# The 64 sample columns of a two-layer recurrent trunk: full 128x128 tiles by writing them twice, and state updates as four K=32 products

## The chip, the cores and the metric

The kernel runs on one core of one Trainium2 chip. The metric is the device time of one execution in microseconds (us); the time before is 3362.74 us, the median of 3 runs (3362.27 to 3363.33). Engines: PE multiplies matrices (PEld loads its stationary operand), DVE and ACT work on vectors, POOL builds masks and issues the DMAs of the states, SP issues the DMAs of the weights.

## The reference

One inference step of a trunk of two layers, in float32. Layer 0 mixes tokens with an mLSTM, layer 1 with HGRN2; each mixer is followed by a SwiGLU of width 5632, with RMSNorm ahead of every part. The prompt has 256 tokens that start from a zero state. The sample has 8 sequences of 8 tokens, each with a state of its own. Cut to what matters here:

```
# mLSTM, 8 heads, per chunk (the sample: one chunk of 8 tokens in each of 8 sequences)
s     = (q . k) * exp(dlog - m_t)                       # causal
num   = s @ v + w_inter * (q @ C)
C_new = decay * C + einsum('bjh,bjhc,bjhv->bhcv', w, k, v)   # (128 x 256) per sequence
# HGRN2, 16 heads
oc    = s @ iv + (q * exp(A)) @ S
S_new = exp(A_last) * S + einsum('bjhc,bjhv->bhcv', k * exp(A_last - A), iv)   # (128 x 128) per sequence
```

So a state update of the sample is, for each head, eight products that each sum over only the 8 tokens of one sequence.

## The kernel before

All 320 tokens (256 of the prompt, 64 of the sample) are columns of tiles with 128 partitions. Every weight matrix is read in tiles of 128 columns, 1 MB each. ACT rounds a tile to a high part `w_hi` (line 303), DVE takes the low part `w_lo` (line 309), and PE makes three products for each of 16 row blocks (lines 319 to 321: hi.hi, hi.lo, lo.hi), 48 in all, 320 columns wide. These are called the big products here. Three tiles after one another keep ACT, DVE and PE busy at once; `w_hi` and `w_lo` have two buffers.

The mixers' own work is laid between the big products. A head of the mLSTM has six weight tiles (slots 0 to 5), a head of HGRN2 four (slots 0 to 3). Behind the big products of a slot PE runs a "tail" of small float32 products. In the loop of the mLSTM these tails are: behind slot 0 `m6` of the head before (sums for the norm, line 1427, and part of the state update, line 1390), behind slot 1 `m7` of the head before (the rest of the update) and `m1` (gate rows of this head spread over 128 partitions by a product with 8 rows of ones, lines 1364 and 1365, and k turned, line 1358), behind slot 3 `m3` (v turned), behind slot 4 `m4` (scores), behind slot 5 `m5` (numerator, denominator, prompt state, first part of the update). In HGRN2 they are: behind slot 0 `h8` and `h4`, behind slot 1 `h5`, behind slot 2 `h6`, behind slot 3 `h7`, which ends with the state update (line 1560), all for the one or two heads before.

Token blocks are 128, 128 and 64 wide. Where the sample's 64 tokens are the stationary operand, PE works with 64 of its columns (a form that the trace writes as `128*64`); where they are summed over, with 64 of its rows (`64*128`). A state update lays k into eight masked copies (`wk_seq`, `hk_seq`; DVE lines 944 and 1224, 1024 elements), multiplies each with v over 64 rows, and DVE adds the eight products to the decayed state (line 966 for C; lines 1232 and 1236 for S).

Each engine runs its instructions in the order of the code and waits on semaphores. `lo_done` releases the big products of a slot, `g_o` tells that `h7` is done, `m_C2` and `g_S` that a head's state may be stored. At the start the arena under `kT` holds `row_m`, which two small DMAs read, so DVE waits for them (`m_stored`) ahead of the first `m_evac`.

Of the kernel before, what the change touches and what calls it, by code (L numbers as in the profile page):

```python
# [19 lines left out]
P = 128  # L20
D = 2048
KT = D // P
TP = 256
NB, TB = 8, 8
TS = NB * TB
T = TP + TS
MH, MDV = 8, 256
# [66 lines left out]
def trunk(nc, x_prompt, x_sample, C_in, n_in, m_in, S_in, norm_mix_g, norm_ffn_g, norm_final_g,  # L94
# [7 lines left out]
    with ExitStack() as ctx:  # L102
# [22 lines left out]
        seq_mask = sb("seq_mask", [TS, NB])  # L125
# [32 lines left out]

        NROWS = 2 * T + NB + TS
# [19 lines left out]
        z_gate, t_gate = carve(T), carve(T)  # L179
        row_b, row_a, row_m, row_w, sum_restart, max_restart = (carve(T) for _ in range(6))  # L180
# [3 lines left out]
        kT, qT = carve(T), carve(T)  # L184
        vT, oT = carve(2, T), carve(2, T)
# [3 lines left out]
        wk_seq = carve(NB, P)  # L189
# [8 lines left out]
        row_of_head = carve(NROWS, parts=MH)  # L198
# [5 lines left out]
        hf, hg, hg_sig, hq, hk, h_logf, hA = (carve(T) for _ in range(7))  # L204
        q_exp, k0, q0, hi_T = (carve(T) for _ in range(4))
        k_exp = h_logf
        pair = carve(2, T)
# [5 lines left out]
        hk_seq = carve(NB, P)  # L213
# [19 lines left out]
        MX = bank[2:8]  # L233

# [27 lines left out]
        m_new0, m_new1, m_new2 = sem("m_new0"), sem("m_new1"), sem("m_new2")  # L262
        m_C0, m_C1, m_C2 = sem("m_C0"), sem("m_C1"), sem("m_C2")
# [9 lines left out]
        g_ikept, g_kkept, g_kseq, g_o, g_sq, g_sum, g_rstd = (sem("g_" + n) for n in ("ikept", "kkept", "kseq", "o", "sq", "sum", "rstd"))  # L273
# [149 lines left out]
        def _(pool):  # L423
# [7 lines left out]
            pool.memset(seq_mask[:, :], 1.0)  # L431
            pool.memset(penal, 0.0)
# [13 lines left out]
            tail = penal[0:TS, TP + P:].rearrange("p (b t) -> p b t", b=NB)  # L446
# [3 lines left out]
                               fill=0.0, base=0, channel_multiplier=1)  # L450
            pool.drain()
            pool.affine_select(out=seq_mask[:, :], in_=seq_mask[:, :], pattern=[[TB, NB]], compare_op=ALU.is_ge,
# [5 lines left out]
            pool.drain()  # L458
            pool.memset(restart[:, 0:TP:SEG], 0.0)
# [41 lines left out]
            def store_C(h):  # L501
                pool.wait_ge(m_C2, h + 1)
# [36 lines left out]
        def _(act):  # L539
# [39 lines left out]
            def m2(h):  # L579

                act.wait_ge(m_turned, h + 1)
                need(act, m_C2, h)
                act.activation(k_tok[:, 0:2, :], MX[2][:, 0:2 * P].rearrange("p (a b) -> p a b", a=2), ACT.Copy)
                act.activation(k_tok[0:TS, 2, :], MX[2][0:TS, 2 * P:3 * P], ACT.Copy)
# [4 lines left out]
                act.activation(att[:, 0:TP + P], att[:, 0:TP + P], ACT.Exp, scale=-1.0)  # L589
                act.activation(att[0:TS, TP + P:], att[0:TS, TP + P:], ACT.Exp, scale=-1.0).then_inc(m_weights, 1)  # L590

            def m4(h):

                act.wait_ge(m_vturned, h + 1)
                for i in range(2):
                    act.activation(v_tok[:, 0:2, i * P:(i + 1) * P],
                                   MX[2 + i][:, 0:2 * P].rearrange("p (a b) -> p a b", a=2), ACT.Copy)
                    last = act.activation(v_tok[0:TS, 2, i * P:(i + 1) * P], MX[2 + i][0:TS, 2 * P:3 * P], ACT.Copy)
                last.then_inc(m_vkept, 1)

            def m6(h):
# [6 lines left out]
                act.activation(vT, hs, ACT.Square).then_inc(m_sq, 1)  # L608
# [121 lines left out]
            def h5(h):  # L730
                act.wait_ge(g_p[0], h + 1)
                act.activation(i_tok[:, 0:2, :], MX[0][:, 0:2 * P].rearrange("p (a b) -> p a b", a=2), ACT.Copy)
                act.activation(i_tok[0:TS, 2, :], MX[0][0:TS, 2 * P:3 * P], ACT.Copy).then_inc(g_ikept, 1)
                pair_exps(h, 1)

            def h6(h):
                act.wait_ge(g_p[1], h + 1)
                act.activation(hk_tok[:, 0:2, :], MX[4][:, 0:2 * P].rearrange("p (a b) -> p a b", a=2), ACT.Copy)
                act.activation(hk_tok[0:TS, 2, :], MX[4][0:TS, 2 * P:3 * P], ACT.Copy).then_inc(g_kkept, 1)
# [74 lines left out]
        def _(dve):  # L814
# [20 lines left out]
            def gate_rows():  # L835
# [20 lines left out]
                for l in range(2):  # L856
                    last = dve.tensor_tensor(bound_cols[:, l, :], bound_cols[:, 2 + l, :], bounds[:, 0, :], ALU.subtract)
                last.then_inc(lb_diff, 1)
                dve.wait_ge(gates_capped, 1)
                dve.tensor_scalar(row_w[0:MH], t_gate[32:32 + MH], -1.0, None, ALU.mult)  # L860
                dve.tensor_scalar(row_a[0:MH], t_gate[0:MH], CAP, None, ALU.mult)
                dve.drain()
                dve.tensor_tensor_scan(row_b[0:MH], sum_restart[0:MH], row_w[0:MH], 0.0, ALU.mult, ALU.add)
                dve.drain()
                dve.tensor_tensor(row_a[0:MH], row_a[0:MH], row_b[0:MH], ALU.subtract)
                dve.drain()
                dve.tensor_copy(row_m[0:MH], row_a[0:MH])
# [12 lines left out]
                                  row_a[0:MH, TP:T].rearrange("p (b t) -> p b t", b=NB),  # L880
                                  M_end.to_broadcast((MH, NB, TB)), ALU.subtract)
# [21 lines left out]
            def keep_gate_columns():  # L903
                dve.wait_ge(rows_turned, 1)
                turned = MX[1][:, 0:2 * 3 * MH].rearrange("p (w b h) -> p w b h", w=2, b=3)
                dve.tensor_copy(gate_cols[:, :, 0:2, :], turned[:, :, 0:2, :])
                dve.tensor_copy(gate_cols[0:TS, :, 2, :], turned[0:TS, :, 2, :]).then_inc(rows_kept, 1)
                dve.drain()

            def evac_scaled(ph, n, out, scale=None, b=None):  # L910

                src = bank[(n if b is None else b)][:, 0:T]
# [751 lines left out]
```

## Time and profile before

| | |
|---|---|
| median of the runs | 3362.74 us |
| span of the profiled execution | 3362.1 us |
| PE busy | 3291.8 us, 98% of the span, 22096 matmuls |
| DVE, ACT, POOL busy | 53%, 34%, 2% |
| mLSTM: a head | 60.6 to 61.8 us, 8 heads |
| HGRN2: a head | 41.85 us, 16 heads |

The runs of the table of times lie 0.2 to 1.2 us above the span of the profiled execution, so that the two are taken as one here. A float32 product is recorded as two MATMULs, called passes here (x2 for one product); a turned block (transpose) as one. The length of one MATMUL in the trace is its latency, 270 to 590 ns, and matmuls overlap; what a group costs PE is the distance from its start to the start of the group behind it, and the text always takes that. The granted clock is given as a share of full speed: 1.00 is 2.4 GHz and 0.50 is 1.2 GHz, and nothing lies between except in a mean.

### The profile page before, as it was taken

Reading aid. Unit: us, or ns where it says so; the run is one execution under the profiler, and the core shown is the slowest. Engines: PE = TensorE matmul, PEld = TensorE weight load, DVE = VectorE, ACT = ScalarE, POOL = GpSimd, SP = SyncE. Lnnn points to the kernel's source line nnn. Section 1 sums busy time; section 2 is a strip of 40 time slices with the busy share of each in tenths; the row PEclk is TensorE's granted clock in tenths of the full one; section 3 lists DMA queues with packets and bytes.
Section 4 is the critical chain, followed back from the end, with each engine's and each line's share of the span. In section 5 each row is a group of like instructions: output and inputs, shape, how many; then the busy total and the mean of one; then the engine's idle time right before and its main releaser. Section 6 shows DMA issues by size and latency. Waiting matters only on the chain.

```text
span 3362.1 us, 54467 instructions
## 1 busy us (share of the span) xinstructions
PE 3291.8 (98%) x22096; PEld 3214.9 (96%) x22096; DVE 1797.2 (53%) x2527; ACT 1158.1 (34%) x1306; POOL 78.6 (2%) x130
## 2 busy tenths in 40 slices
PE   7999999999999999999999999998999999999998
PEld 6999998999999999999999999988999999999998
DVE  6455454555534553455666666674555445544554
ACT  4233233333223322224444444443433223222233
POOL 2000000000000000000000000000000000000000
PEclk9999999999999999999999999998999999999999
DMA  5445444555555555555544444453555555555544
GB/s 135 140 114 165 126 129 139 138 150 150 150 150 150 149 150 150 146 142 144 145 127 126 126 126 126 126 139 89 150 150 150 150 150 150 149 150 148 149 132 116
DMA packets 856557, 470.10 MB, mean 140 GB/s; under 512 B 10424, under 2 KB 846144, under 8 KB 856480
## 3 DMA queue, kind: packets, MB, share of 16 engines
q1 hardware_dynamic: 846144, 433.22, 47.2%
q0 software_dynamic: 10144, 35.74, 3.4%
q8 instruction: 55, 0.90, 0.1%
q14 instruction: 22, 0.18, 0.0%
q10 hardware_dynamic: 192, 0.06, 0.0%
HBM read 447.46 MB, written 21.53 MB: 139 GB/s over the span
## 4 chain that ended last, share of the span: by engine, by line
PE 91%; DVE 3%; ACT 2%; DVEq 1%; DMA 1%; issue 1%; SPq 0%; ACTq 0%; POOL 0%; POOLq 0%
PE bank L319 28%; PE bank L321 27%; PE bank L320 27%; PE bank L1509 2%; DVE w_lo L309 2%; ACT w_hi L303 1%; PE bank L1390 1%; PE bank L1560 1%; PE bank L1404 1%; DVEq L1234 1%; PE bank L1548 0%; PE bank L1384 0%; DMA out_dram<-arena 0%; DVE arena L1236 0%; DVE arena L1179 0%
## 5 line engine op out<-in xcount | busy, mean ns | idle before, releaser
L319 PE MATMUL bank<-h_hi,w_hi 128*128 128x320 f32 x4608 | 1455.5, 316 | 13.5 <-DVE w_lo L309 12.3
L321 PE MATMUL bank<-h_hi,w_lo 128*128 128x320 f32 x4608 | 1428.5, 310 | 0.0
L320 PE MATMUL bank<-h_lo,w_hi 128*128 128x320 f32 x4608 | 1428.5, 310 | 0.0
L309 DVE TENSOR_TENSOR w_lo<-raw,w_hi 128x2048 fp32r<-128x2048 f32 (+1 forms) x416 | 935.6, 2249 | 494.8 <-ACT w_hi L303 494.8
L303 ACT ACTIVATE w_hi<-raw 128x2048 fp32r<-128x2048 f32 (+1 forms) x416 | 780.0, 1875 | 760.4 <-PE bank L321 756.7
L319 PEld LDWEIGHTS bank<-h_hi,w_hi 128*128 128x128 f32 x4608 | 870.1, 189 | 27.1 <-DVE w_lo L309 16.9
L320 PEld LDWEIGHTS bank<-h_lo,w_hi 128*128 128x128 f32 x4608 | 870.3, 189 | 0.2
L321 PEld LDWEIGHTS bank<-h_hi,w_lo 128*128 128x128 f32 x4608 | 869.4, 189 | 0.0
L319 PE MATMUL bank<-g_hi,w_hi 128*128 128x320 f32 x1920 | 599.8, 312 | 13.0 <-DVE w_lo L309 6.6
L320 PE MATMUL bank<-g_lo,w_hi 128*128 128x320 f32 x1920 | 596.0, 310 | 0.0
L321 PE MATMUL bank<-g_hi,w_lo 128*128 128x320 f32 x1920 | 596.0, 310 | 0.0
L914 DVE TENSOR_TENSOR arena<-bank,rstd 128x320 f32<-128x320 f32 x264 | 129.5, 490 | 479.4 <-PE bank L321 467.9
L319 PEld LDWEIGHTS bank<-g_hi,w_hi 128*128 128x128 f32 x1920 | 363.2, 189 | 17.0 <-DVE w_lo L309 7.6
L320 PEld LDWEIGHTS bank<-g_lo,w_hi 128*128 128x128 f32 x1920 | 363.1, 189 | 0.0
L321 PEld LDWEIGHTS bank<-g_hi,w_lo 128*128 128x128 f32 x1920 | 362.9, 189 | 0.0
L682 ACT ACTIVATE arena<-arena 128x320 f32<-128x320 f32 x88 | 41.6, 472 | 490.8 <-DVEq L1086 490.8
L1050 DVE TENSOR_TENSOR x<-x,bank 128x320 f32 (+1 forms) x128 | 62.4, 488 | 242.2 <-PE bank L321 242.2
L339 ACT ACTIVATE h_hi<-x,gains (+1 forms) x64 | 36.0, 563 | 205.5 <-DVEq L1055 195.2
L1509 PE MATMUL bank<-arena 128*128 128x128 f32 (+1 forms) x576 | 84.0, 281 | 0.1
L1509 PEld LDWEIGHTS bank<-arena 128*128 128x128 f32 (+1 forms) x576 | 69.7, 180 | 11.2 <-DVE arena L1156 0.3
L1164 DVE COPY_PREDICATED arena<-level_mask,bank 128x256 f32<-128x256 int8 x112 | 50.6, 452 | 34.9 <-PE bank L1509 27.9
L349 DVE SCALAR_TENSOR_TENSOR h_lo<-x,gains,h_hi (+1 forms) x64 | 35.3, 551 | 50.1 <-ACT h_hi L339 50.0
(280 smaller groups left out, 1780.5 us busy)
## 6 DMA issues: line engine op xcount, KB each, us to landing
raw<-in_ffn_w_up_dram SPq DMA_DIRECT2D x176, 1024.0 KB, 5.7
raw<-in_ffn_w_down_dram SPq DMA_DIRECT2D x64, 1024.0 KB, 6.0
raw<-in_hgrn_w_in_dram SPq DMA_DIRECT2D x64, 1024.0 KB, 6.5
raw<-in_mlstm_w_in_dram SPq DMA_DIRECT2D x48, 1024.0 KB, 5.9
raw<-in_ffn_w_down_dram SPq DMA_DIRECT2D x32, 768.0 KB, 5.1
raw<-in_mlstm_w_out_dram SPq DMA_DIRECT2D x16, 1024.0 KB, 6.1
raw<-in_hgrn_w_out_dram SPq DMA_DIRECT2D x16, 1024.0 KB, 6.1
raw<-in_state_mlstm_C_dram POOLq DMA_DIRECT2D x8, 1024.0 KB, 8.8
```

The source lines that it names most:

```text
L303: act.activation(w_hi[:, s % 2, 0:ph.k * P], raw[:, s % ph.ring, 0:ph.k * P], ACT.Copy).then_inc(hi_done, 1)
L309: dve.tensor_tensor(w_lo[:, s % 2, 0:ph.k * P], raw[:, s % ph.ring, 0:ph.k * P], w_hi[:, s % 2, 0:ph.k * P].bitcast(F32), ALU.subtract).th ...
L319: pe.matmul(out, tile_hi, hi[:, k, :], start=(k == 0), stop=False)
L320: pe.matmul(out, tile_hi, lo[:, k, :], start=False, stop=False)
L321: last = pe.matmul(out, tile_lo, hi[:, k, :], start=False, stop=(k == ph.k - 1))
L339: act.activation(h_hi[:, bass.ds(j, 1), :], x[:, bass.ds(j, 1), :], ACT.Copy, scale=gains[:, bass.ds(NORM_GAIN[r] + j, 1)]).then_inc(x_hi_ ...
L349: dve.scalar_tensor_tensor(h_lo[:, bass.ds(j, 1), :], x[:, bass.ds(j, 1), :], gains[:, bass.ds(NORM_GAIN[r] + j, 1)], h_hi[:, bass.ds(j, 1 ...
L682: act.activation(f_sig[:, (s - 1) // 2, :], fa[:, (s - 1) // 2, :], ACT.Sigmoid).then_inc(f_sig_done, 1)
L914: return dve.tensor_tensor(out, src, rstd[:, :], ALU.mult)
L1050: add = dve.tensor_tensor(x[:, bass.ds(j, 1), :], x[:, bass.ds(j, 1), :], bank[s % ph.banks][:, 0:T].rearrange("p (a t) -> p a t", a=1), A ...
L1164: dve.copy_predicated(scores[:, 0:TP], level_mask[:, li, 0:TP], MX[mx][:, 0:TP])
L1509: last = pe.matmul(MX[mx][0:c1 - c0, c0:c1], left[:, c0:c1], right[:, c0:c1], start=True, stop=True)
```

## The change

The sample's columns are written twice into the tiles of k, v, `hk`, `k0`, `pair` and i, so that the third token block is 128 wide (64 tokens and the same 64 again, or zeros). Every small product then uses all 128 rows and columns. Where the second copy would be summed as well, the masked weights or scores are zero there. The gate rows are spread from a tile with 128 partitions of which 120 are zero.

The state update no longer masks k eight times. The 128 rows of the third block are taken as four quarters of 32 rows, that is of four sequences; a quarter holds two sequences that it serves. v (or i) is laid out twice side by side, each copy masked by `half_mask` to one of the two, and one product over 32 rows gives the updates of both sequences, 512 (or 256) columns wide. The four products read different quarters of the rows and write different PSUM banks. `m7` on PE is gone, the whole update of C stands in `m6`. DVE adds decay and product in one instruction for each sequence in HGRN2 too. `row_m` lies elsewhere, and DVE waits for `m_stored` only after the loop.

```diff
-        wk_seq = carve(NB, P)
+        v_half = carve(2 * MDV)
-        row_of_head = carve(NROWS, parts=MH)
+        row_of_head = carve(NROWS)
+        row_m = carve(T)
+        NEW_C, NEW_S = (0, 2, 3, 5), (0, 1, 2, 3)
+        def group(g):
+            return slice(32 * g, 32 * g + 32)
+        def sequence(g, u):
+            return 4 * (g % 2) + 2 * (g // 2) + u
...
+            def evac_twice(out, b, scale=None):
+                evac_scaled(out[:, 0:T], b, scale)
+                return evac_scaled(out[:, T:TW], b, scale, slice(TP, T))
...
             def m5(h):      # DVE
+                for u in range(2):
+                    last = dve.tensor_scalar(v_half[:, u * MDV:(u + 1) * MDV], v_tok[:, 2, :], half_mask[:, u:u + 1], None, ALU.mult)
...
-                    if s == 1 and isinstance(it, int):
-                        dve.wait_ge(m_stored, 32)
...
             def m1(h):      # PE
-                pe.matmul(MX[0][:, 0:R_EM], ones[0:MH, :], row_of_head[:, 0:R_EM], start=True, stop=True)
+                pe.matmul(MX[0][:, 0:R_EM], ones[:, :], row_of_head[:, 0:R_EM], start=True, stop=True)
...
-            def new_C(mx, b0):
-                for i in range(2):
-                    last = pe.matmul(MX[mx][:, i * MDV:(i + 1) * MDV], wk_seq[0:TS, b0 + i, :], v_tok[0:TS, 2, :],
-                                     start=True, stop=True)
+            def new_C():
+                for g in range(ROW_GROUPS):
+                    last = pe.matmul(MX[NEW_C[g]][:, 0:2 * MDV], wk[group(g), 2, :], v_half[group(g), :], start=True, stop=True)
...
             def m6(h):      # PE
-                pe.wait_ge(m_C0, h + 1)
-                new_C(4, 2)
-                new_C(5, 4).then_inc(m_new1, 1)
-            def m7(h):
-                pe.wait_ge(m_C1, h + 1)
-                new_C(4, 6).then_inc(m_new2, 1)
+                pe.wait_ge(m_vhalf, h + 1)
+                need(pe, m_C1, h)
+                new_C().then_inc(m_new1, 1)
...
             def h7(h):      # PE
-                for b in range(NB):
-                    last = pe.matmul(MX[(0, 2)[b // 4]][:, b % 4 * P:(b % 4 + 1) * P], hk_seq[0:TS, b, :], i_tok[0:TS, 2, :],
-                                     start=True, stop=True)
+                for g in range(ROW_GROUPS):
+                    last = pe.matmul(MX[NEW_S[g]][:, 0:2 * P], hk_tok[group(g), 2, :], i_half[group(g), :], start=True, stop=True)
...
             def h8(h):      # DVE
-                dve.tensor_tensor(S, S, q_exp[:, TP + TB - 1:T:TB].rearrange("p (b a) -> p b a", a=1).to_broadcast((P, NB, P)),
-                                  ALU.mult)
-                dve.drain()
-                for i, mx in enumerate((0, 2)):
-                    last = dve.tensor_tensor(S[:, 4 * i:4 * i + 4, :], S[:, 4 * i:4 * i + 4, :],
-                                             MX[mx][:, :].rearrange("p (b v) -> p b v", b=4), ALU.add)
+                for g in range(ROW_GROUPS):
+                    for u in range(2):
+                        b = sequence(g, u)
+                        end = TP + b * TB + TB - 1
+                        last = dve.scalar_tensor_tensor(S[:, b, :], S[:, b, :], q_exp[:, end:end + 1],
+                                                        MX[NEW_S[g]][:, u * P:(u + 1) * P], ALU.mult, ALU.add)
```

Where instructions move, on PE in the loop of the mLSTM: the tails behind slot 0 and slot 1. A row is a line of the code with its operands and the output's partitions x columns. First before, line 1390 being the state update:

```order
L1427 MATMUL bank<-arena,ones 128x320 x2
L1390 MATMUL bank<-arena 128x256 x4
...
L1390 MATMUL bank<-arena 128x256 x2
L1362 REGISTER_ALU
L1364 MATMUL bank<-arena,ones 128x392
L1365 MATMUL bank<-arena,ones 128x320
L1358 MATMUL bank<-ident,arena 128x128 x2
L1358 MATMUL bank<-ident,arena 64x128
```

and the same place in the changed program, where line 1428 is the state update:

```order
L1463 MATMUL bank<-arena,ones 128x320 x2
L93 REGISTER_ALU
L1428 MATMUL bank<-arena 128x512 x4
...
L1397 REGISTER_ALU
L1400 MATMUL bank<-arena,ones 128x392
L1401 MATMUL bank<-arena,ones 128x320
L1393 MATMUL bank<-ident,arena 128x128 x3
```

The update of the tail behind slot 1 is gone, the one behind slot 0 has four products of 512 columns where four of 256 stood (two more stood in `m5`), and the turned block of 64 partitions is one of 128.

On DVE, the place in the loop of HGRN2 that runs when `h7` is done, before (`h8` and the start of `h4`):

```order
L914 TENSOR_TENSOR arena<-bank,rstd 128x320
L309 TENSOR_TENSOR w_lo<-raw,w_hi 128x2048
L1231 COPY arena<-bank 128x128
L1232 TENSOR_TENSOR arena<-arena 128x1024
L1236 TENSOR_TENSOR arena<-arena,bank 128x512 x2
L1179 SCALAR_TENSOR_TENSOR arena<-restart,arena 128x320
```

and after:

```order
L938 TENSOR_TENSOR arena<-bank,rstd 128x320
L938 TENSOR_TENSOR arena<-bank,rstd 128x64
L325 TENSOR_TENSOR w_lo<-raw,w_hi 128x2048
L1262 COPY arena<-bank 128x128
L1267 SCALAR_TENSOR_TENSOR arena<-arena,bank 128x128 x8
L1209 SCALAR_TENSOR_TENSOR arena<-restart,arena 128x320
```

Eight instructions of 128 elements stand where three of 1024, 512 and 512 stood.

## Rows read from the trace of the kernel before

**Rows 1.** The page: span, and busy time of the engines.
```profile
span 3362.1 us, 54467 instructions
PE 3291.8 (98%) x22096; PEld 3214.9 (96%) x22096; DVE 1797.2 (53%) x2527; ACT 1158.1 (34%) x1306; POOL 78.6 (2%) x130
```
**Rows 2.** Waits of PE (who waited for whom: total us, times, longest).
```profile
PE bank L1364 <- DVE arena L930: 7.4, 1, 7.4
```
**Rows 3.** Timeline of DVE at the start (start us, us, operation, [idle before]).
```profile
65.67 0.49 DVE L915 SCALAR_TENSOR_TENSOR arena<-bank,rstd 128x320 f32<-128x320 f32 x1 [4.16 <-DMA out_dram<-arena]
```
**Rows 4.** Timeline of PE, HGRN2, tail behind slot 3.
```profile
1754.13 0.39 PE L1554 MATMUL bank<-arena 128*128 128x128 f32 x2
1754.36 0.39 PE L1555 MATMUL bank<-arena 128*128 128x128 f32 x2
1754.67 0.43 PE L1556 MATMUL bank<-arena 64*128 64x64 f32 x2
1755.03 0.71 PE L1558 MATMUL bank<-arena 128*128 128x128 f32 x4
1755.68 2.05 PE L1560 MATMUL bank<-arena 64*128 64x128 f32 x16
1757.65 0.42 PE L319 MATMUL bank<-h_hi,w_hi 128*128 128x320 f32 x1
```
**Rows 5.** Timeline of PE, HGRN2, tail behind slot 2.
```profile
1742.39 2.67 PE L1509 MATMUL bank<-arena 128*128 128x128 f32 x18
1744.98 0.42 PE L319 MATMUL bank<-h_hi,w_hi 128*128 128x320 f32 x1
```
**Rows 6.** Timeline of PE, mLSTM, tail behind slot 5.
```profile
229.09 0.59 PE L1384 MATMUL bank<-arena,ones 128*128 128x256 f32 x2
235.52 0.41 PE L319 MATMUL bank<-h_hi,w_hi 128*128 128x320 f32 x1
```
**Rows 7.** Timeline of PE, mLSTM, state update behind slot 0.
```profile
243.83 1.99 PE L1390 MATMUL bank<-arena 64*128 64x256 f32 x8
245.75 0.41 PE L319 MATMUL bank<-h_hi,w_hi 128*128 128x320 f32 x1
```
**Rows 8.** Timeline of PE, mLSTM, tail behind slot 1.
```profile
252.99 1.13 PE L1390 MATMUL bank<-arena 64*128 64x256 f32 x4
254.04 0.92 PE L1364 MATMUL bank<-arena,ones 8*128 8x392 f32 x2
254.81 0.70 PE L1365 MATMUL bank<-arena,ones 8*128 8x320 f32 x2
255.74 0.39 PE L319 MATMUL bank<-h_hi,w_hi 128*128 128x320 f32 x1
```
**Rows 9.** Timelines of DVE, ACT and PE in slot 2 of the same head.
```profile
254.15 0.87 DVE L966 SCALAR_TENSOR_TENSOR raw<-raw,spread,bank 128x256 f32<-128x256 f32 x2 [0.41 <-PE bank L1390]
256.02 0.39 ACT L583 ACTIVATE arena<-bank 128x256 f32<-128x256 f32 x1 [9.21 <-PE bank L1358]
263.15 0.41 PE L319 MATMUL bank<-h_hi,w_hi 128*128 128x320 f32 x1
```
**Rows 10.** Windows (A:B, length, PE busy, granted clock, DMA share, GB/s).
```profile
193.70:197.10 3.40, 3.40 (x14) 0.50 1.04 293
242.66:263.15 20.49, 20.36 (x122) 1.00 0.52 160
180.85:202.61 21.76, 21.76 (x122) 0.92 0.49 151
```
**Rows 11.** Timelines of DVE and PE, HGRN2, slot 0.
```profile
1758.07 1.22 DVE L1232 TENSOR_TENSOR arena<-arena 128x1024 f32<-128x1024 f32 x1
1760.57 0.82 DVE L1179 TENSOR_TENSOR_SCAN arena<-restart,arena 128x320 f32<-128x320 f32 x1
1765.58 2.29 DVE L309 TENSOR_TENSOR w_lo<-raw,w_hi 128x2048 fp32r<-128x2048 f32 x1 [0.90 <-ACT w_hi L303]
1767.93 0.41 PE L319 MATMUL bank<-h_hi,w_hi 128*128 128x320 f32 x1 [0.64 <-DVE w_lo L309]
```

More of the change, by code:

```diff
@@ L26 @@
 T = TP + TS
+ROW_GROUPS = 4
+TW = T + TS
 MH, MDV = 8, 256
@@ L431, in _ @@
             pool.memset(seq_mask[:, :], 1.0)
+            pool.memset(quarters, 1.0)
             pool.memset(penal, 0.0)
@@ L450, in _ @@
                                fill=0.0, base=0, channel_multiplier=1)
+            starts = [[-80, 2], [-32, 2], [-TB, 2]]
+            pool.affine_select(out=quarters, in_=quarters, pattern=starts, compare_op=ALU.is_ge,
+                               fill=0.0, base=0, channel_multiplier=1)
             pool.drain()
+            pool.affine_select(out=quarters, in_=quarters, pattern=[[-step, n] for step, n in starts], compare_op=ALU.is_ge,
+                               fill=0.0, base=TB - 1, channel_multiplier=-1)
             pool.affine_select(out=seq_mask[:, :], in_=seq_mask[:, :], pattern=[[TB, NB]], compare_op=ALU.is_ge,
@@ L1348, in rows_to_columns @@
                 for which, row in ((0, row_a), (1, row_w)):
-                    for b, n in enumerate((P, P, TS)):
-                        last = pe.transpose(MX[1][0:n, which * 3 * MH + b * MH:which * 3 * MH + (b + 1) * MH],
-                                            row[0:MH, b * P:b * P + n], ident[0:MH, 0:MH])
+                    for b in range(3):
+                        src = row[0:MH, b * P:(b + 1) * P]
+                        last = pe.transpose(MX[1][:, which * 3 * MH + b * MH:which * 3 * MH + (b + 1) * MH],
+                                            src, ident[0:MH, 0:MH])
                 last.then_inc(rows_turned, 1)
             def turn(mx, src, inc=None):
-                for b, n in enumerate((P, P, TS)):
-                    last = pe.transpose(MX[mx][0:n, b * P:(b + 1) * P], src[:, b * P:b * P + n], ident[:, :])
+                for b in range(3):
+                    part = src[:, b * P:(b + 1) * P]
+                    last = pe.transpose(MX[mx][:, b * P:(b + 1) * P], part, ident[:, :])
                 return last
@@ L1445, in m_body @@
                         m6(before)
-                    if s == 1 and before is not None:
-                        m7(before)
                     if s in (1, 3, 4, 5):
@@ L1508, in level_products @@
                     if c0 < w:
-                        last = pe.matmul(MX[mx][0:c1 - c0, c0:c1], left[:, c0:c1], right[:, c0:c1], start=True, stop=True)
+                        keys = left[:, c0:c0 + P]
+                        last = pe.matmul(MX[mx][:, c0:c1], keys, right[:, c0:c1], start=True, stop=True)
                 return last
```

199 lines of the change are left out of this document (104 added, 95 removed).

## The prediction

> **What bounds the kernel now.** I read the page first: PE is busy for 98% of the span [rows 1]. So this change pays where it shortens what PE does, or ends one of the few waits of PE. The page's busy time can't say what a small product costs, since matmuls overlap. For that I read PE's timeline and take distances from start to start. Then I asked at each slot whether the big products behind a tail start because PE is free or because `w_lo` has come.
>
> The reader is to see three things. First, a full 128x128 pass costs 0.11 us (L1554 to L1555, two passes in 0.23), and so do the 64-row passes of L1560 (16 in 1.97, less what follows); a change of shape costs extra. L1555's two passes take 0.31 to the 64-row L1556, 0.09 over 0.22; L1556's take 0.36, 0.14 over; L1558's four full ones 0.65 for 0.45; L1560's sixteen 1.97 for 1.79 [rows 4]. Each change of form costs some 0.19 us, half ahead of the first pass and half ahead of the second. Second, the mLSTM is bound by PE, but slot 3 at 263.15 starts just as a chain ends that runs from the turned k over ACT's copies and table load, `w_hi` and `w_lo`; ACT starts it at 256.02 [rows 9]. Third, HGRN2's slot 1 starts 0.64 us after PE was free, and the chain is DVE's and ACT's from `h7`'s end at 1757.65 to 1767.93 [rows 4, 11]. At the start PE waits 7.4 us for the gate rows, and inside it DVE waits 4.16 us for a DMA [rows 2, 3].
>
> **The change part by part.** A pass of up to 128 columns is 0.112 us. A 256-column one is 0.216, (1.92 - 0.19)/8 from L1390 x8 [rows 7]; one of 392 is 0.33, (0.77 - 0.10)/2 [rows 8]. From these two a 512-column pass is 0.43, an estimate.
>
> *HGRN2, slot 2.* 18 passes in 2.59 us [rows 5] hold three blocks with 64 columns. All full: 18 x 0.112 = 2.02. Gain 0.57 a head. Slot 1 has one such block of three: a third of that, less 0.07 for passes that the wider stationary operand brings from 0.09 to 0.11: 0.12.
>
> *HGRN2, slot 3.* From L1554 to the end 3.52 us. Ahead of the update stand then ten full passes (L1554, 1555, 1556, 1558): 1.12. The update has 4 products of 2 passes, 256 columns, over 32 rows; the trace shows no 32-row product in another quarter than the one before it. Upper bound: they run one behind the other like L1390's eight passes, 1.92 + 0.09 for the change of form. That gives 3.13, a gain of 0.39. Lower bound: products on different quarters of the rows run side by side. The two passes of one product use the same quarter and stay in order, passes start in order, so pass 2 of one runs beside pass 1 of the next: five steps for eight, 5 x 0.216 + 3 x 0.03 + 0.28 = 1.45. Total 2.57, gain 0.95. I take the lower: the four banks and the four quarters are separate, and nothing else orders them. 15 heads run so.
>
> *HGRN2, slot 0.* From `h7`'s end to slot 1 are 10.28 us, of which PE waits 0.64 [rows 4, 11]; its own side is at most 9.64. As long as the chain stays above that, only the chain counts. It holds L1232 and two L1236, 2.50 us from 1758.07 to 1760.57; after it eight instructions of 128 elements. A 256-element one of that kind steps 0.39 (two in 0.87, the last 0.48 long) [rows 9]; DVE takes 1.04 ns an element (2048 in 2.29, 1024 in 1.22 [rows 11]), so 0.26 for 128; 8 x 0.26 = 2.06. Gain 0.44, 14 times. Were there no overlap between them, 0.34 each, it would be a loss of 0.24. The second copy of `k0`, 0.13 to 0.22 us, lies beside ACT: DVE waits 0.90 us for `w_hi` behind it [rows 11]. The second copy of i comes ahead of `g_o`, where DVE idles. After that the chain is 9.84. HGRN2: 15 x (0.57 + 0.12 + 0.95) + 14 x 0.44 = 30.8.
>
> *mLSTM, slots 3 to 5.* `m5` takes 6.43 us [rows 6]. After: three times 2 x 0.216 + 4 x 0.112 = 0.88 for the causal products, 0.22 for `qn`, 0.86 and 0.40 and 0.22 for the prompt's state, n and the sample's n, 4.34. Gain 2.09, part of it the piece of the update that moves to `m6`. `m4` has one 64-column block, gain 0.13; the two turned blocks of `m3` cost 0.08 more, an estimate. 2.14 x 8 = 17.1.
>
> *mLSTM, tails behind slots 0 and 1.* Behind slot 0: 1.92 [rows 7] becomes 0.19 + X. One behind the other X is 8 x 0.43 = 3.44, a loss of 1.71; side by side 5 x 0.43 + 0.08 = 2.23, a loss of 0.50. Behind slot 1: 2.75 + 0.09 [rows 8] becomes 2 x 0.33 + 2 x 0.27 + 3 x 0.11 = 1.53, gain 1.31. PE would gain 0.81. But then the wait for slot 3 grows. Now ACT's chain is released by `m_C1`: DVE is free at 253.74 [rows 9], 0.13 later with the second copy of k, and makes four instructions of 0.39 instead of two: 255.5. From there 7.13 us as before, less 0.15 for two merged ACT copies: 262.5 for 263.15. I take 0.7, and 7 heads make 4.9. In the other case PE is the later one (263.25): a loss of 0.1 each.
>
> *The clock.* In 4 of the 6 heads between 119.05 and 487.51 a stretch of 3.4 us runs at 0.50, right behind the tail of slot 1 with its 64-row and 8-row products: the same part of a head takes 21.76 us with it and 20.49 without [rows 10]. Half of that tail goes and the rest uses all rows, so I expect these stretches gone: 4 x 1.27 and 0.3 for a later, partly hidden one, 5.4.
>
> *The start and the ends.* DVE's 4.16 us wait goes off the path; against it stand 0.25 for second copies in the gate rows and 0.2 for that of k: 3.7 gained. The memset of `row_of_head` hides under ACT's gate functions. Head 0's `m1`: 0.3. In the last mLSTM head DVE no longer waits for a second set of products before the state may be stored and the tile under C loaded: 1.3. The last heads of HGRN2 wait on the same chains as slot 0, twice: 1.5, an estimate.
>
> Sum: 30.8 + 17.1 + 4.9 + 5.4 + 3.7 + 0.3 + 1.3 + 1.5 = 65.0. The profiled execution's 3362.1 us less this are 3297.1; the median of the runs stands 0.6 above that execution: **3298 us**.
>
> **The rivals.**
>
> *One behind the other.* The 32-row products don't overlap. For it: every pass in the trace waits its turn, even when the form is the same. Against it: those all use the same rows. HGRN2 gains 15 x (0.57 + 0.12 + 0.39) + 6.2 = 22.4, the mLSTM 17.1 - 0.7, the rest 12.2: 51, or **3312 us**; if 3.7 us of 32-row passes behind slot 0 also keep a half-rate stretch of 1.27 in each of seven heads, 3320.
>
> *Closer packing.* The first passes of all four products run together and then the second ones, two steps for five: 3 x 0.216 = 0.65 less in each HGRN2 head, 15 x 0.65 = 9.7. The mLSTM gains nothing further, its slot 3 waits for `m_C1`'s chain. **3288 us**. For it: nothing but the code's order ties pass 2 of one product ahead of pass 1 of the next. Against it: in every group of the trace passes start in the order in which they are issued. The Trainium skill, page "TensorE: Matmul & The Clock Gate", section "Measured speedup vs the span model", gives 3.07x for four K=32 products of 512 columns, where my five steps for eight are 1.6x; no row before the change shows it, and by it the time would be near this rival's.
>
> *Slower.* The clock. A 32-row block of 3.7 us in each mLSTM head and one of 2.0 in each HGRN2 head bring PE's clock to 0.50 for stretches like the one of [rows 10], where each costs up to 1.7. With nothing overlapping and the old stretches gone the gain is 51; 30 stretches more eat it. Two in each of 22 heads are 75: **3386 us**. For it: the stretch behind slot 1 follows narrow products. Against it: the 64-row block of 1.92 behind slot 0 [rows 7] is followed by full clock in the same head [rows 10], and HGRN2's update never lowers it.
>
> *DVE's eight instructions don't overlap*, 0.34 each: slot 0 loses 0.24 instead of gaining 0.44, 14 x 0.68 = 9.5 us: **3307 us**.
>
> **How the numbers follow.** Forecast 0.55; one behind the other 0.2; closer packing 0.1; DVE's eight 0.1; slower 0.03; the rest, no change, 0.02. The forecast's own range is 3291 to 3305, from the clock (5), the start (2 either way, as PE's idle time there is also followed by half rate) and the ends. For 8 in 10 the range goes from 3286, past closer packing, to 3318, over the serial case. A measurement tells 0.2%, 6.7 us, from no change. Faster takes all cases but two: 0.96; same 0.01; slower 0.03.
>
> **What the profile would show.** The update in HGRN2: four products from first start to big product, 1.45 us if side by side, 2.0 if not; start distances within a product of 0.216, between products of 0.03 or 0.216. In slot 2, 18 passes in 2.02. A head of HGRN2 in 39.8 us. The chain of slot 0 at 9.84 us with a wait of some 0.2 left over. In the mLSTM the update in 2.4 us, a wait of DVE's `w_lo` ahead of slot 3 in every head, heads of 57.8 us, clock 1.00 throughout. At the start a wait of PE of 3.7 us instead of 7.4. I am wrong if the passes step by 0.216 throughout, if a full third block costs more than 0.112 a pass, or if DVE or ACT come late in slots 1 to 3 of HGRN2, where PE doesn't wait for them now.

## The result, and the profile after

The changed kernel takes 3282.86 us, the median of 4 runs (3280.78 to 3284.13), beside 3363.0 for the kernel before (4 runs, 3362.27 to 3363.33): a ratio of 0.9761, with a 95% interval of 0.9748 to 0.9774. The forecast was 3298 with a range of 3286 to 3318: the direction was right and the gain, 80 us, larger than the range allowed. The profiled execution went from 3362.1 to 3279.3 us, by 82.8 where the sum said 65.0.

The page of the changed kernel, span and busy time, which answers to [rows 1]:

```profile
span 3279.3 us, 54117 instructions
PE 3201.8 (98%) x21904; PEld 3152.9 (96%) x21904; DVE 1778.3 (54%) x2619; ACT 1155.3 (35%) x1242; POOL 79.2 (2%) x135
```

PE is still the bound at 98%, with 192 fewer matmuls of 22096. Most of the gain is thus in the distances between matmuls, not in their number. Timeline of PE, HGRN2, the tail behind slot 3 (start us, length us, then the instruction), which answers to [rows 4]:

```profile
1633.53 0.38 PE L1583 MATMUL bank<-arena 128*128 128x128 f32 x2
1633.75 0.39 PE L1584 MATMUL bank<-arena 128*128 128x128 f32 x2
1633.97 0.39 PE L1585 MATMUL bank<-arena 128*128 128x128 f32 x2
1634.20 0.33 PE L1586 MATMUL bank<-arena 128*128 128x64 f32 x2
1634.37 0.66 PE L1588 MATMUL bank<-arena 128*128 128x128 f32 x4
1634.96 0.71 PE L1590 MATMUL bank<-arena 32*128 32x256 f32 x8
1635.61 0.41 PE L335 MATMUL bank<-h_hi,w_hi 128*128 128x320 f32 x1
```

L1590 is the state update: eight passes of 256 columns fit between 1634.96 and 1635.61, 0.65 us. Passes that queue behind one another start 0.216 us apart at this width; such a distance is called a step here, and eight steps would be 1.73. Two more terms: a quarter is 32 of the 128 rows, and a change of form is the place where PE goes from products over 128 rows to products over 32 or back. Two narrower cuts of the same timeline show how they lie:

```profile
1634.96 0.50 PE L1590 MATMUL bank<-arena 32*128 32x256 f32 x4
...
1635.28 0.39 PE L1590 MATMUL bank<-arena 32*128 32x256 f32 x4
```

The four first passes all start at 1634.96 (within 0.02 us), the four second ones at 1635.28. From L1584 to the big product are 1.86 us, where before L1554 to L319 took 3.52 [rows 4]: a gain of 1.66, and the prediction had 0.95. The tail behind slot 2, which answers to [rows 5], is a timeline of PE as well:

```profile
1661.55 2.12 PE L1538 MATMUL bank<-arena 128*128 128x128 f32 x18
1663.48 0.39 PE L335 MATMUL bank<-h_hi,w_hi 128*128 128x320 f32 x1
```

It is 1.93 us long, where it was 2.59 and 2.02 was forecast. Slot 0 of HGRN2, timelines of DVE and, in the last line, of PE, which answer to [rows 11]:

```profile
1636.06 2.15 DVE L1267 SCALAR_TENSOR_TENSOR arena<-arena,bank 128x128 f32<-128x128 f32 x8
1638.12 0.82 DVE L1209 TENSOR_TENSOR_SCAN arena<-restart,arena 128x320 f32<-128x320 f32 x1
...
1643.13 2.29 DVE L325 TENSOR_TENSOR w_lo<-raw,w_hi 128x2048 fp32r<-128x2048 f32 x1 [0.77 <-ACT w_hi L319]
...
1645.48 0.42 PE L335 MATMUL bank<-h_hi,w_hi 128*128 128x320 f32 x1 [0.36 <-DVE w_lo L325]
```

DVE's eight instructions step by 0.26 us (2.06 for all), as forecast, and from the end of `h7` (1635.61) to slot 1 (1645.48) are 9.87 us against 10.28 before; 9.84 was forecast. The timeline writes a wait of 0.36 for PE.

The mLSTM: the update behind slot 0, and the tail behind slot 5, timeline of PE, which answer to [rows 7] and [rows 6]:

```profile
215.56 0.59 PE L1421 MATMUL bank<-arena,ones 128*128 128x256 f32 x2
...
219.86 0.39 PE L335 MATMUL bank<-h_hi,w_hi 128*128 128x320 f32 x1
...
228.15 0.71 PE L1428 MATMUL bank<-arena 32*128 32x512 f32 x4
...
228.68 0.61 PE L1428 MATMUL bank<-arena 32*128 32x512 f32 x4
229.22 0.42 PE L335 MATMUL bank<-h_hi,w_hi 128*128 128x320 f32 x1
```

`m5` takes 4.30 us (4.34 forecast, 6.43 before). The whole update of C takes 1.07 us, again two steps. Slots 2 and 3 of the same head, timelines of ACT, DVE and PE, which answer to [rows 9]:

```profile
239.98 0.49 ACT L608 ACTIVATE arena<-bank 128x384 f32<-128x384 f32 x1 [8.84 <-DVE raw L997]
...
240.80 1.28 ACT L610 ACT_TABLE_LOAD   x1
...
242.69 1.90 ACT L319 ACTIVATE w_hi<-raw 128x2048 fp32r<-128x2048 f32 x1
...
244.63 2.29 DVE L325 TENSOR_TENSOR w_lo<-raw,w_hi 128x2048 fp32r<-128x2048 f32 x1 [1.47 <-ACT w_hi L319]
...
238.37 0.41 PE L335 MATMUL bank<-h_hi,w_hi 128*128 128x320 f32 x1 [0.32 <-DVE w_lo L325]
...
246.97 0.42 PE L335 MATMUL bank<-h_hi,w_hi 128*128 128x320 f32 x1 [1.30 <-DVE w_lo L325]
```

DVE's update of C (L997) releases ACT at 239.98; three copies, a table load and an exponential stand ahead of ACT's `w_hi` for slot 3, and DVE's `w_lo` follows it. By the timeline PE has been free for 1.30 us when slot 3 starts. The waits of PE for the whole program (who waited for whom: total us, times, longest) say the same: before, `w_lo` cost PE 18.9 us in 18 waits, now more.

```profile
PE bank L335 <- DVE w_lo L325: 28.6, 32, 4.2
...
PE bank L1400 <- DVE arena L962: 3.5, 1, 3.5
```

The second row answers to [rows 2]: 7.4 us became 3.5. Last the windows of PE (A:B, length, PE busy, granted clock, DMA share, GB/s), a whole mLSTM head, the six behind it and the start:

```profile
111.28:169.30 58.02, 56.30 (x384) 1.00 0.52 148
169.30:514.65 345.35, 335.63 (x2283) 1.00 0.51 145
63.10:66.50 3.40, 3.40 (x8) 0.50 0.49 61
```

The half-rate stretches of [rows 10] are gone from the seven mLSTM heads between the first and the last mark of the table below. Behind the gate rows at the start 3.4 us still run at 0.50; before it was 10.2 us:

```profile
64.00:74.20 10.20, 7.50 (x23) 0.50 0.31 68
```

Read by the marks of the timeline (first product of the norm's sums in each head) the 82.8 us lie as follows. The forecast column is the prediction's terms, sorted by the same marks; eight heads have seven stretches between their marks, sixteen have fifteen.

| stretch | before | after | gained | forecast |
|---|---|---|---|---|
| to the first mLSTM mark | 119.05 | 111.28 | 7.8 | 6.1 |
| 7 mLSTM heads | 429.36 | 403.37 | 26.0 | 25.3 |
| to the first HGRN2 mark | 1132.69 | 1128.10 | 4.6 | 2.9 |
| 15 HGRN2 heads | 615.98 | 572.25 | 43.7 | 30.6 |
| rest | 1065.02 | 1064.3 | 0.7 | 0 |

Most of the miss, 13.1 of 17.8 us, is in HGRN2, whose head went from 41.85 to 38.85 us. The first and the third row are known less well than the others. Six traces of kernels whose instructions up to the first mLSTM mark are the same (this one, q0000, q0011, q0101, k128 and narrow below) reach it between 108.26 and 111.28 us. The third row's stretch takes 1127.72 to 1130.03 us in three traces with the same instructions in it (this one, stored and rows8). One trace tells these two rows to 2 or 3 us only.

### The profile page after: what moved, and what is told of

Read it like the earlier page. It is cut to its first block, busy times and chain, and to the rows that moved or that the text cites. A ratio compares the mean times of both kernels' runs of the same rounds, so it can differ in the third digit from the quotient of the medians.

```text
span 3279.3 us, 54117 instructions
## 1 busy us (share of the span) xinstructions
PE 3201.8 (98%) x21904; PEld 3152.9 (96%) x21904; DVE 1778.3 (54%) x2619; ACT 1155.3 (35%) x1242; POOL 79.2 (2%) x135
## 4 chain that ended last, share of the span: by engine, by line
PE 90%; DVE 5%; ACT 3%; issue 1%; DMA 1%; DVEq 0%; SPq 0%; ACTq 0%; POOL 0%; POOLq 0%
PE bank L335 28%; PE bank L337 27%; PE bank L336 27%; DVE w_lo L325 2%; PE bank L1538 2%; ACT w_hi L319 1%; DVE arena L1267 1%; PE bank L1441 1%; PE bank L1577 0%; DVE raw L997 0%; PE bank L1421 0%; DVE arena L1209 0%; PE bank L1590 0%; DMA arena<-in_mlstm_w_in_dram 0%; PE bank L1357 0%
## 5 line engine op out<-in xcount | busy, mean ns | idle before, releaser
L319 ACT ACTIVATE w_hi<-raw 128x2048 fp32r<-128x2048 f32 (+1 forms) x416 | 780.3, 1876 | 746.3 <-PE bank L337 741.0
L938 DVE TENSOR_TENSOR arena<-bank,rstd 128x320 f32<-128x320 f32 (+1 forms) x296 | 133.5, 460 | 486.0 <-PE bank L337 476.0
L1538 PE MATMUL bank<-arena 128*128 128x128 f32 (+1 forms) x576 | 73.0, 277 | 0.0
L1538 PEld LDWEIGHTS bank<-arena 128*128 128x128 f32 x576 | 69.5, 194 | 0.0
L1196 DVE COPY_PREDICATED arena<-level_mask,bank 128x320 f32<-128x320 int8 (+1 forms) x112 | 55.0, 491 | 24.1 <-PE bank L1538 16.7
```

Of the source, the lines that this page charges most:

```text
L319: act.activation(w_hi[:, s % 2, 0:ph.k * P], raw[:, s % ph.ring, 0:ph.k * P], ACT.Copy).then_inc(hi_done, 1)
L938: return dve.tensor_tensor(out, src, rstd[:, cols], ALU.mult)
L1196: dve.copy_predicated(scores[:, 0:w], level_mask[:, li, 0:w], MX[mx][:, 0:w])
L1538: last = pe.matmul(MX[mx][:, c0:c1], keys, right[:, c0:c1], start=True, stop=True)
```

## Experiments

**Which products overlap.** If quarters of the rows are what lets the four products run at once, putting two or all four on the same quarter must bring steps back, and full rows must bring all eight. In all four kernels of this group only the operands' rows change, in both updates (L1428 and L1590), so the instructions and the work around them stay. The new states of the sample then lack some of their sums or have sums of other sequences in them. The diff shows the two operands of the product alone.

```diff
-    wk[group(g), 2, :], v_half[group(g), :]             # and the same for hk_tok, i_half
+    wk[group(0), 2, :], v_half[group(0), :]             # q0000
+    wk[group(g // 2), 2, :], v_half[group(g // 2), :]   # q0011
+    wk[group(g % 2), 2, :], v_half[group(g % 2), :]     # q0101
+    wk[:, 2, :], v_half[:, :]                           # k128
```

> The changed kernel, but all four 32-row products of both state updates read rows 0 to 31 (so the new states are wrong sums; everything else is computed). Theory A, packing: products on different quarters of the rows run at the same time, products on the same quarter one behind the other. Then HGRN2's update takes 0.19 + 8 x 0.216 = 1.92 us instead of 0.64, 15 x 1.28 = 19 us more; the mLSTM's 0.19 + 8 x 0.43 = 3.6 instead of 1.07, of which 1.9 us a head are hidden by the waits ahead of slots 2 and 3, so 7 x 0.6 = 4 us more; in all 3283 + 23 = 3306. Rival B: a 32-row pass is short wherever it reads, the quarters don't matter: 3283, HGRN2's update stays at 0.64. Rival C: in addition the clock drops to 0.50 behind the 3.6 us block in the mLSTM: some 7 us on top, 3313.

> The changed kernel, but products 0 and 1 read rows 0 to 31 and products 2 and 3 rows 32 to 63 (wrong sums in the new states). Theory A with free order: what counts is how many passes share a quarter, four here: 4 steps of 0.216, HGRN2's update 1.05 to 1.15 us, 15 x 0.43 = 6.5 us more, 3289. Rival D, the order of issue counts: pass starts stay in order, products 2 and 3 can't begin until product 1's last pass has: 7 steps, 1.8 us, 15 x 1.1 = 17 more, 3300.

> As the run before, with quarters 0, 1, 0, 1. Theory A with free order: four passes on each of two quarters, 4 steps, the same 3289. Rival D, order of issue: the pairs stand well here; if the passes of a product are issued one behind the other, 0a 0b 1a 1b, product 1 begins beside 0b: 7 steps for the eight passes, if all first passes of a pair go out before the second ones, 4 steps. A difference between this run and the one before shows that order counts, none that it doesn't.

> The changed kernel, but the four products of both updates read all 128 rows (wrong sums in the new states): full tiles without quarters, no change of form anywhere in the loops. Theory A: HGRN2's update 8 x 0.216 = 1.73 us ahead of the big products, against 0.64 and 0.12 for changes of form: 15 x 1.0 = 15 us more. mLSTM: 3.44 against 1.16, less 1.9 that the waits hide: 7 x 0.4 = 3 us more. 3301; and 5 us less than the run with all products on quarter 0, by the changes of form. Rival B: as fast as the changed kernel.

Measured: q0000 3306.67 us (ratio 0.9834, 0.9818 to 0.9851), q0011 3289.93 (0.9782, 0.9765 to 0.9798), q0101 3288.11 (0.9778, 0.9761 to 0.9794), k128 3301.39 (0.9819, 0.9802 to 0.9835), the kernel before 3361.77 on the same chip. In q0000 the second pass starts 0.32 us behind the first, the six others 0.216 apart, and the big product 0.31 behind the last. Timelines of PE around the update, q0000:

```profile
1719.88 1.99 PE L1590 MATMUL bank<-arena 32*128 32x256 f32 x8
1721.80 0.41 PE L335 MATMUL bank<-h_hi,w_hi 128*128 128x320 f32 x1
```

q0011, whole and in a narrow cut that holds only the first starts:

```profile
1717.26 1.14 PE L1590 MATMUL bank<-arena 32*128 32x256 f32 x8
1718.33 0.42 PE L335 MATMUL bank<-h_hi,w_hi 128*128 128x320 f32 x1
...
1717.26 0.49 PE L1590 MATMUL bank<-arena 32*128 32x256 f32 x2
```

and k128:

```profile
1719.33 1.89 PE L1590 MATMUL bank<-arena 128*128 128x256 f32 x8
1720.87 0.49 PE L335 MATMUL bank<-h_hi,w_hi 128*128 128x320 f32 x1
```

The block is 0.65 us on four quarters, 1.07 on two and 1.92 on one. With 0.216 for a step these are 2, 4 and 8 steps and each time some 0.2 for the change of form inside the block (0.43 + 0.2, 0.86 + 0.2, 1.73 + 0.2). So the products of one quarter queue among themselves, and products of different quarters start within 0.02 us of each other. Two quarters take the same time in the order 0,0,1,1 and in the order 0,1,0,1. In q0011 two passes start together at 1717.26; passes of one quarter can't (q0000), so the second is of the third product or the fourth, and it starts ahead of the second product. The order in the code isn't what decides.

k128 has eight steps without a change of form, but its 1.54 us read too short. The big product starts 0.03 behind the last pass there, and the second big product 0.33 behind the first, where 0.25 lie between them in q0000. From the start of L1588, the group ahead of the update, to the second big product are 2.38 us in k128 and 2.76 in q0000: the change of form to 32 rows and the one back cost 0.39 together. The block's own distance holds 0.2 of that, the groups on either side the rest. k128 also shows what packing as such is worth over a kernel with full rows: 18.5 us by the medians of the two kernels, beside which the kernel before took 3361.77 and 3363.0. HGRN2's heads take 38.85, 39.27, 40.1 us (4, 2, 1 quarters) and 39.9 (k128).

**What the mLSTM's update is worth.** In q0000 the update of C takes 2.56 us longer as well (3.63 for 1.07), yet a head of the mLSTM is only 0.7 us longer (58.43 for 57.7): the waits ahead of slots 2 and 3 take it up. Two kernels try that. order_mh takes the waits away by order alone; all work is kept. ACT makes the `w_hi` of slot 3 before it copies the turned k and loads its table, DVE the `w_lo` of slot 3 before its scaling of k, and in HGRN2 ACT makes the `w_hi` of slot 1 between `h8` and `h4`.

```diff
             (mLSTM, ACT)
-                    if s == 2:
+                    if s == 3:
                         m2(it)
             (mLSTM, DVE: m2 moved from behind m_evac of s == 2 to ahead of that of s == 3)
+                    if s == 3:
+                        m2(it)
             (HGRN2, ACT)
+                    if early is not None:
+                        early()        # split_high(act, H_IN, it, 1), between h8 and h4
```

> The changed kernel with two steps moved; nothing is left out. In the mLSTM ACT rounds the tile of slot 3 ahead of m2, and DVE takes its low part ahead of m2. In HGRN2 ACT rounds the tile of slot 1 behind h8 and ahead of h4, where it idles 3.9 us. Theory: the changed kernel waits for w_lo ahead of slot 3 of the mLSTM (1.46 us a head) and ahead of slot 1 of HGRN2 (0.5 us a head) because w_hi comes late: 7 x 1.4 + 14 x 0.5 = 17 us less, 3266. Rival: something else, DVE's own work, is next in line at once, and under half of it shows: 3275 or more.

order_mh takes 3262.62 us (3260.51 to 3263.3), a ratio of 0.9702 (0.9686 to 0.9719): 20 us below the changed kernel, and the fastest here. Waits and timeline of PE:

```profile
PE bank L335 <- DVE w_lo L325: 14.1, 11, 4.2
```
```profile
335.58 0.43 PE L1468 MATMUL bank<-arena,ones 128*128 128x320 f32 x1
...
346.96 0.41 PE L335 MATMUL bank<-h_hi,w_hi 128*128 128x320 f32 x1 [0.31 <-DVE w_lo L325]
...
391.78 0.43 PE L1468 MATMUL bank<-arena,ones 128*128 128x320 f32 x1
```

An mLSTM head takes 56.20 us (57.7 in the changed kernel), an HGRN2 head 38.22 (38.85). What stays in the mLSTM is a wait of 0.31 ahead of slot 2. In these traces the seven mLSTM heads are 10.7 us shorter in sum and the fifteen of HGRN2 8.8. Each head gains more than the wait that the timeline wrote (1.49 for 1.30, 0.63 for 0.36), since the written wait begins at the modelled end of the last pass, and a big product can start before that. The second kernel, order_qM, is order_mh with the update of C on rows 0 to 31 for all four products, so that C lacks three quarters of the sample's sums.

> The reordered changed kernel (order_mh), with the mLSTM's state update alone put on rows 0 to 31 for all four products (so that the sample's new C lacks three quarters of its sums); HGRN2's update is untouched. Theory A, once the waits ahead of slots 2 and 3 are gone, the packing of the mLSTM's update counts in full: the block takes some 3.6 us instead of 1.07, 2.5 us a head less at most 0.3 us of wait that remains, for 7 heads, so 16 to 18 us over order_mh: 3278 to 3281 us, heads of 58.4 to 58.8 us. Theory B, the update of C still ends ahead of a chain on DVE and ACT that sets slot 3: heads stay near 56.2 us and the time at 3261 to 3266 us.

It takes 3278.56 us (3275.16 to 3282.46), 16 more than order_mh. Timeline and windows of PE:

```profile
292.15 3.69 PE L1433 MATMUL bank<-arena 32*128 32x512 f32 x8
295.78 0.42 PE L335 MATMUL bank<-h_hi,w_hi 128*128 128x320 f32 x1
```
```profile
112.80:119.60 6.80, 6.80 (x22) 0.50 0.34 94
174.30:181.10 6.80, 6.80 (x23) 0.50 0.28 75
235.70:239.10 3.40, 3.40 (x12) 0.50 0.49 128
```

The block is 3.63 us, and heads at full clock take 58.08, 1.88 more than 56.20; of the 2.56 more in the block the wait ahead of slot 2, now gone, hides most of the rest. So packing counts in the mLSTM once nothing waits. The total came out as expected and its make-up didn't: heads are shorter than the 58.4 to 58.8 of the expectation, and three of them run 3.4 or 6.8 us at 0.50 right behind the long 32-row block (heads of 61.2, 61.2 and 59.7), which the expectation didn't have.

**Parts of the change one by one.** Three kernels undo one part each: `stored` puts the wait for `m_stored` back ahead of the first `m_evac`, `rows8` spreads the gate rows with products over 8 rows again, and `narrow` gives the third block of the level products (L1538) its 64 columns back. Of the two products of rows8 the diff shows the first.

```diff
+                    if s == 1 and isinstance(it, int):
+                        dve.wait_ge(m_stored, 32)                         # stored
...
-                pe.matmul(MX[0][:, 0:R_EM], ones[:, :], row_of_head[:, 0:R_EM], start=True, stop=True)
+                pe.matmul(MX[0][:, 0:R_EM], ones[0:MH, :], row_of_head[0:MH, 0:R_EM], start=True, stop=True)   # rows8
...
-                        keys = left[:, c0:c0 + P]
-                        last = pe.matmul(MX[mx][:, c0:c1], keys, right[:, c0:c1], start=True, stop=True)
+                        keys = left[:, c0:c1]                             # narrow
+                        last = pe.matmul(MX[mx][0:c1 - c0, c0:c1], keys, right[:, c0:c1], start=True, stop=True)
```

> The changed kernel with DVE's wait for m_stored back ahead of its first m_evac; nothing is left out. Theory: this is what shortened the start. DVE waits again some 4 us for the small DMA, PE starts m1 3.7 us later. If that is all, 3283 + 3.7 = 3287. Rival: PE's idle time there also sets the clock: the stretches at 0.50 grow from 3.4 us to 10.2 as before the change, 3.4 us more, 3290. Rival: the DMA wait was hidden, 3283.

> The changed kernel with the two products of m1 over 8 rows again; nothing is left out. Theory: the 3.4 us stretches at 0.50 in 4 mLSTM heads came from the whole tail behind slot 1, 1.06 us of 64-row state products and 1.4 us of 8-row products; with the 8-row ones alone they stay away. The tail gets 0.4 us longer, which the wait ahead of slot 2 (0.48) hides: 3283. Rival: the 8-row products alone bring the half-rate stretches back, 4 x 1.3 = 5 us more, 3288.

> The changed kernel with the third block of the HGRN2 level products 64 columns wide again; nothing is left out. Theory: what the full tiles save in slots 1 and 2 is the change of form. Slot 2's tail goes from 1.92 to 2.59 us and slot 1's from 1.81 to 1.95: 15 x 0.8 = 12 us more, 3295. Rival: these slots end with w_lo from DVE and not with PE, and the longer tail disappears into slack: 3283 to 3286.

stored: 3287.6 us (0.978, 0.9763 to 0.9796). PE's wait for the gate rows is 6.2 us again for 3.5, 6.8 us behind it run at 0.50 for 3.4, and the first mLSTM mark comes at 115.88 for 111.28, which would make this part worth 4.6; by the medians it is 4.7. Not all of it need be the edit: the trace of stored has 3.4 us at 0.50 at 45.0 us as well, ahead of the gate rows, and the changed kernel's hasn't, and the mark moves by some 3 us between traces in any case. rows8: 3279.88 (0.9754, 0.9737 to 0.977), no slower than the changed kernel, heads of 57.68, and no half-rate stretch in them: full rows for the gate rows are worth nothing here once the 64-row update is gone. narrow: 3297.23 (0.9806, 0.979 to 0.9823), 14.4 above the changed kernel. Timeline of PE of narrow, the tail behind slot 2:

```profile
1743.36 2.66 PE L1538 MATMUL bank<-arena 128*128 128x128 f32 x18
1745.95 0.42 PE L335 MATMUL bank<-h_hi,w_hi 128*128 128x320 f32 x1
```

That is 2.59 us, the value of before [rows 5], for 1.93. A head takes 39.77 us for 38.85; 0.92 x 15 = 13.8.

**One part alone in the kernel before.** rows8 left open what had brought the half-rate stretches of [rows 10]. b_full is the kernel before with only `row_of_head` on 128 partitions (zeroed once by a memset) and the two products of `m1` over all of them; the 64-row update stays.

```diff
-        row_of_head = carve(NROWS, parts=MH)
+        row_of_head = carve(NROWS)
...
-                pe.matmul(MX[0][:, 0:R_EM], ones[0:MH, :], row_of_head[:, 0:R_EM], start=True, stop=True)
+                pe.matmul(MX[0][:, 0:R_EM], ones[:, :], row_of_head[:, 0:R_EM], start=True, stop=True)
```

> One part of the change alone, put into the kernel before: the gate rows lie in a tile of 128 partitions, 120 of them zero, and the two products that spread them run over all 128 rows; nothing else is changed. Theory A, the half-rate stretches behind slot 1 of the mLSTM follow the products over 8 rows: the four stretches of 3.4 us (132, 194, 317 and 378 us) vanish, 4 x 1.2 to 1.4 us, and a change of form fewer gives some 0.1 us a head more: some 3357 us (3355 to 3359). Theory B, they follow the 64-row update products or the whole tail: the stretches stay and the time is that of before, 3361 to 3363 us. The run of the changed kernel with 8-row products had no such stretch either, which speaks against A being needed there.

It takes 3355.2 us (10 runs, 3353.33 to 3358.41) beside 3363.6, a ratio of 0.9978 (0.9969 to 0.9988). Windows of PE over all seven heads:

```profile
117.45:177.94 60.49, 60.36 (x392) 1.00 0.50 142
177.94:540.02 362.08, 361.32 (x2331) 1.00 0.49 138
```

All four stretches are gone with this part alone. So is a fifth, which the trace before has at 500.93 to 504.34 us, in the last of the seven heads, at 0.50. They are gone too in rows8, which has the 8-row products but no 64-row update ahead of them. So the drop was seen only where both stood behind slot 1, the 64-row update and the 8-row products right after it. q0000 (3.63 us of 32-row products, one stretch in seven heads) and order_qM (three) point the same way, and k128, with the same passes over all rows, has none. This is one trace of each kernel; why such a tail is followed by half rate, and why not in every head, stays open. The seven heads gain 6.8 us in sum: 1.3 in each of the five with a stretch and 0.15 in each of the other two, so that a stretch costs 1.15. Ahead of the first mark come 1.6.

## Why the prediction was off, step by step

**The failed step is the packing of the update**: "The two passes of one product use the same quarter and stay in order, passes start in order, so pass 2 of one runs beside pass 1 of the next: five steps for eight". The first part held (q0000: same quarter, 0.216 apart), the second did not: products of different quarters don't keep the order of the code (q0011). It takes two steps, the rival called closer packing, which had a chance of 0.1. The argument against it, that passes start in the order in which they are issued in every group, came from groups that all use the same rows, so it said nothing on this case. The block was forecast at 1.45 and takes 0.65. Three steps less are 0.65 of the 0.8; the rest is that the sum had 0.37 for the form and the starts between products, where 0.22 were measured. Ahead of the block stand 1.21 us where the sum had 1.12, so that the whole tail gained 0.71 more than forecast: 0.71 x 15 = 10.7 us, the largest part of the miss of 17.8. The Trainium skill's figure, 3.07x for four K=32 products on page "TensorE: Matmul & The Clock Gate", section "Measured speedup vs the span model", bears on this: a reader who had gone by it would have taken the packed case. Here one quarter takes 3.63 us and four take 1.07 for 512 columns, 3.4x, and 1.92 and 0.65 for 256 columns, 3.0x: the trace is near the page's figure.

**Full tiles in HGRN2** were right in kind and a little small: slot 2 gained 0.66 a head (0.57 forecast) and slot 1 0.21 (0.12). The sum put 0.112 on each pass of a full third block. That is the price of 128 moving columns, and the third block still has 64: two such passes take 0.17 together (L1586: 1634.20 to 1634.37). narrow shows the part by itself: 0.92 a head.

**HGRN2's slot 0** came as forecast: 0.41 for 0.44, with DVE's eight instructions at 0.26 each. The wait left over is 0.36 for 0.2.

**The mLSTM** was right in its sum, 26.0 for 25.3, in part because errors cancel, and the packing error didn't show there. Behind slot 0 the update was forecast at 2.4 and takes 1.07, but slot 3 is bound by the chain from `m_C1` over ACT and DVE, as the prediction said. That cover is shown by q0000 (2.56 us more work in the block, 0.7 more in the head) and by order_qM (1.88 more once the waits are gone). From a head's mark to slot 3 are 19.99 us where 20.49 stood, a gain of 0.50 for 0.7. Behind it a head gained 2.4 to 2.5 for 2.14: `m5` 2.13 for 2.09, `m4` 0.21 for 0.13, `m3` nothing where a loss of 0.08 stood, and 0.1 in slot 4. A head of 57.8 was forecast; it takes 57.7.

**The clock.** The stretches went, as forecast, and 5.4 us was near: 5 x 1.15 = 5.8 by the heads of b_full. The parts were less right. A stretch costs 1.15 by the length of a head, not 1.27, and the fifth, in the last head, gave as much as the others where the sum had 0.3 for a later one. The prediction named the narrow tail as a whole; b_full and rows8 show heads without a stretch when either the 8-row products or the 64-row update ahead of them is gone. The slower rival's mechanism exists, but only where the 32-row products run one behind the other (q0000: 1.6 us in one head; order_qM: 7.8 us over three heads); packed, they are over in 1.07 us and no head shows it.

**The start** gained 7.8 for 6.1. The edit of the wait gave some 4.6 (stored) where 3.7 stood, and the half-rate stretch behind the gate rows shrank from 10.2 to 3.4 us. That the shorter wait shrank it is likely but not shown: PE's wait and the stretch are 8.2 and 10.2 us in b_full, 7.4 and 10.2 before, 6.2 and 6.8 in stored, 3.5 and 3.4 in the changed kernel, but 3.5 and 6.8 in rows8. Head 0's `m1` gave up to 1.6 (b_full) where 0.3 stood. Neither difference stands out of the 3 us by which traces differ there, and the whole lies within the "2 either way" that the prediction gave the start.

**The ends** were too small as well: 4.6 for 2.9 between the last mLSTM mark and the first HGRN2 one, of which 0.9 is head 0's share of closer packing and the full blocks; the rest is within what traces of like kernels differ by in this stretch, so the term of 1.3 for the last mLSTM head is neither shown nor refuted. The 0.7 of the last stretch wasn't taken apart. The last two heads of HGRN2 gained 1.75 and 3.0, 1.2 more than forecast.

The range failed at its low end, since it was cut at 3286 on the packing rival with nothing added for the other terms, though the prediction itself gave the start 2 us either way. With the packing and the full blocks at what was measured (0.71 and 0.18 a head more than in the sum, 13 us), the forecast would have stood near 3284, 2 us from the measured time.

## What to carry to other kernels

Products of K=32 on the four quarters of the rows, with their own PSUM banks, run at the same time here: count the passes of the fullest quarter, whatever the order in the code, and add the change of form. Where each engine runs a list by its order, look next at what the shorter tail uncovers: here a change in the order of ACT's and DVE's work was worth 20 us more on top of 80. About half of that were waits for `w_lo` in the mLSTM that the shorter tails had opened (0.13 us ahead of slot 3 before, 1.30 after); the other half lay in HGRN2, where PE waited ahead of slot 1 before the change too. An order seen among instructions that share a resource says nothing about those that don't.

## What the runs showed of the hardware

- A change of form (rows in use) costs some 0.2 us, and a block between full tiles has two: from the group ahead to the second big product are 2.76 us in q0000 and 2.38 in k128. Of this the block's own distance holds 0.2: 0.65, 1.07 and 1.92 us for 2, 4 and 8 steps of 0.216, and 1.07 and 3.63 for 2 and 8 steps of 0.43.
- Products on different quarters of the rows start out of the code's order: with quarters 0,0,1,1 a product of the second quarter starts within 0.02 us of the first product, and the second product waits its turn (q0011).
- A third block with 64 stationary columns costs more than a full one: 18 passes in 2.59 us for 1.93.
- 3.63 us of 32-row products are followed by 3.4 us at half rate in one of seven heads (q0000) or by 3.4 to 6.8 us in three of seven (order_qM); the same rows in 1.07 us, and the same passes over all rows (k128), in none.
